# Moving the first two weight pieces of every stage into the stage before, in a two-block transformer kernel on one Trainium2 core

## The reference

```python
x = x + 0.5 * (1.0 + mod[:, 0, 2]) * swiglu(pre(x, 0), ffn_wi[l, 0], ffn_wo[l, 0])
h = pre(x, 1)                       # rmsnorm(x) * g * (1 + scale) + shift
y = hgrn2_mixer(h, ...)             # or diff_attention_mixer, or nsa and gmlp merged
x = x + (1.0 + mod[:, 1, 2]) * y
x = x + 0.5 * (1.0 + mod[:, 2, 2]) * swiglu(pre(x, 2), ffn_wi[l, 1], ffn_wo[l, 1])
```

## Time and profile before

| | us |
|---|---|
| median of 3 runs | 2288.79 |
| lowest and highest run | 2288.27, 2292.33 |
| span of the profiled execution (first to last instruction) | 2286.7 |
| PE busy in it | 2177.3 |
| DVE busy | 1624.0 |
| ACT busy | 1062.8 |

### The profile page before, as it was taken

How to read it: one execution, slowest core, us unless ns; L and a number is a source line. 1 busy time by engine, 2 the same in 40 slices (tenths; PEclk the granted TensorE clock), 3 DMA queues, 4 the chain that set the end, 5 groups by cost and what they waited for, 6 DMA issues and landing times.

```text
span 2286.7 us, 29523 instructions
## 1 busy us (share of the span) xinstructions
PE 2177.3 (95%) x10588; PEld 1802.0 (79%) x10588; DVE 1624.0 (71%) x2258; ACT 1062.8 (46%) x1265; POOL 0.2 (0%) x4
## 2 busy tenths in 40 slices
PE   3999989999999996899999999999999999999998
PEld 2888987788788875788888887778878888777887
DVE  6777767777788785677677866577767776656545
ACT  3344533443534465434443446653354344665334
POOL 0000000000000000000000000000000000000000
PEclk9999999999999997999999999999999999999999
DMA  7899624688688651487678853459867886334553
GB/s 308 317 334 318 218 82 156 231 319 312 228 327 315 226 193 65 149 330 292 229 284 306 315 201 129 131 185 338 302 214 279 309 317 217 129 129 148 191 195 129
DMA packets 128228, 537.20 MB, mean 235 GB/s; under 512 B 15024, under 2 KB 15760, under 8 KB 109200
## 3 DMA queue, kind: packets, MB, share of 16 engines
q1 hardware_dynamic: 128144, 536.06, 65.5%
HBM read 534.90 MB, written 1.10 MB: 234 GB/s over the span
## 4 chain that ended last, share of the span: by engine, by line
PE 87%; DVE 8%; ACT 3%; issue 1%; DMA 1%; SPq 0%; DVEq 0%; ACTq 0%
PE GU L1633 14%; PE GU L1637 14%; PE GU L1635 14%; PE PY L1633 11%; PE PY L1637 11%; PE PY L1635 11%; DVE wL L909 3%; PE TM L1677 2%; ACT wH L517 1%; PE PY L1941 1%; PE PY L2057 1%; ACT M L569 1%; ACT xH L564 1%; DMA M<-in_ada_t 1%; PE PY L1644 1%
## 5 line engine op out<-in xcount | busy, mean ns | idle before, releaser
L909 DVE TENSOR_TENSOR wL<-raw,wH 128x2048 fp32r<-128x2048 f32 x344 | 776.4, 2278 | 232.2 <-ACT wH L517 231.0
L517 ACT ACTIVATE wH<-raw 128x2048 fp32r<-128x2048 f32 x344 | 645.3, 1900 | 149.6 <-PE PY L1637 81.2
L1633 PE MATMUL GU<-wH,xH 128*128 128x512 f32 (+1 forms) x1584 | 628.2, 397 | 34.0 <-DVE xL L1033 30.6
L1637 PE MATMUL GU<-wH,xL 128*128 128x512 f32 (+1 forms) x1584 | 616.3, 389 | 0.0
L1635 PE MATMUL GU<-wL,xH 128*128 128x512 f32 (+1 forms) x1584 | 615.1, 388 | 0.0
L1633 PEld LDWEIGHTS GU<-wH,xH 128*128 128x128 f32 x1584 | 298.3, 188 | 100.1 <-issue 27.4
L1637 PEld LDWEIGHTS GU<-wH,xL 128*128 128x128 f32 x1584 | 298.1, 188 | 62.8
L1635 PEld LDWEIGHTS GU<-wL,xH 128*128 128x128 f32 x1584 | 298.7, 189 | 57.0
L597 ACT ACTIVATE hH<-TM 128x512 fp32r<-128x512 f32 x80 | 47.9, 598 | 587.7 <-PE TM L1677 587.6
L922 DVE CUSTOM_DVE_ANT_0 ada<-ada,cond 128x1024 f32<-128x1024 f32 x272 | 316.6, 1220 | 0.0
L1633 PE MATMUL PY<-wH,hH 128*128 128x512 f32 x640 | 198.6, 392 | 0.9 <-DVE wL L909 0.9
(11 more groups left out here) (288 smaller groups left out, 1888.1 us busy)
## 6 DMA issues: line engine op xcount, KB each, us to landing
raw<-in_up_w SPq DMA_DIRECT2D x352, 512.0 KB, 6.1
ada<-in_ada_t SPq DMA_DIRECT2D x136, 1024.0 KB, 7.8
raw<-in_down_w SPq DMA_DIRECT2D x176, 512.0 KB, 4.8
raw<-in_c_w SPq DMA_DIRECT2D x96, 512.0 KB, 4.4
raw<-in_a_w SPq DMA_DIRECT2D x40, 512.0 KB, 4.6
raw<-in_b_w SPq DMA_DIRECT2D x32, 512.0 KB, 4.5
M<-in_ada_t SPq DMA_DIRECT2D x8, 1024.0 KB, 12.3
gB<-gates SPq DMA_DIRECT2D x12, 512.0 KB, 6.0
```

The costliest lines, as they stand in the source:

```text
L517: act.activation(wH[:, to, 0:words], raw[:, slot, 0:words], ACT.Copy).then_inc(s_high, 1)
L909: dve.tensor_tensor(wL[:, to, 0:words], raw[:, slot, 0:words], wH[:, to, 0:words], ALU.subtract).then_inc(s_split, 1)
L1633: pe.matmul(outs[i], aH, wh[i], start=first, stop=False)
L1637: ins = pe.matmul(outs[i], aL, wh[i], start=False, stop=last)
```

## The change

The first two pieces of a stage get buffers of their own in the arena, `firstH` and `firstL` (two of each, at word 3072 of `M` and up). Their loads, and both cuts, are issued in the preceding stage. For a feed-forward that is one piece in each of its last two turns, for a mixer its end. At the boundary no piece of the new stage is cut any more in tile 0's part. PE turns tile 0 of x inside the last matmuls of the preceding stage (between the halves of `down_last(1)`, or after a quarter of the last tile of a mixer's projection), and tile 1 after group d = 6 instead of 5. DVE does tile 0's modulation before tile 1's `output`, and puts the two halves of that `output` between the blocks of tile 0's `xL`. Since mixers 2 and 3 load other weights into the same words of the arena, that load now also waits until the first two pieces have been used, and stands one piece later.

```diff
+FIRST_AT = 3 * D
+        arena_at = nc.sbuf_base - 4 * ARENA
+        firstH, firstL = ([nc.alloc_sbuf_tensor_at(f"first{part}{q}", [P, PIECE], F32R,
+                                                   offset=arena_at + 4 * (FIRST_AT + (2 * q + k) * PIECE))
+                           for q in range(2)] for k, part in enumerate("HL"))
...
@@ SP: the mixers' other weights
             def load_compression(i):
                 sp.wait_ge(s_x, NT * (3 * i + 7))
+                sp.wait_ge(s_eaten, first_eaten(i + 2))
...
-                    if l > 1 and n == 4:
+                    if l > 1 and n == 5:
                         load_compression(l - 2)
@@ SP: the last two turns of a feed-forward
-                if turns < NF - 1:
-                    loop(1 + turns, NF - 1 - turns, 0)
+                    loop(1, NF - 3, turns > 0)
+                for q in range(2):
+                    c = NF - 2 + q
+                    load_up(l, j, c, 0)
+                    if turns >= c:
+                        load_ada(c0 + c - 1, 0)
+                    if after(l, j):
+                        load_first(after(l, j), q)
+                    load_up(l, j, c, 1)
+                    if turns >= c:
+                        load_ada(c0 + c - 1, 1)
+                    load_down(l, j, c - 1)
                 gate_out(l, j)
                 load_down(l, j, NF - 1)
@@ ACT: a first piece, no wait for a slot of wH
+            def cut_first(q):
+                slot = t.next("piece") % RING
+                act.wait_ge(s_raw[slot], t.next(s_raw[slot], 32))
+                act.activation(firstH[q][:, :], raw[:, slot, :], ACT.Copy).then_inc(s_high, 1)
@@ ACT: norm, at a boundary
+                if before:
+                    squares(0)
+                    root(0)
                 for i in range(NT):
-                    if before:
-                        squares(i)
-                        root(i)
-                    if before and i == 0:
-                        cut(early=before == "ffn")
...
+                    if before and i == 0:
+                        squares(1)
+                        root(1)
@@ ACT: ffn (DVE alike)
                 loop(NF - 3)
+                if after(l, j):
+                    cut_first(0)
                 cut()
                 hidden_high()
...
+                if after(l, j):
+                    cut_first(1)
                 cut()
                 cut()
                 cut_last()
                 hidden_high()
-                if (l, j) != PHASES[-1]:
-                    cut(early=1)
@@ DVE: boundary, tile i
+                    low(0)
+                    low(1)
+                    if before and i == 0:
+                        wait_output_1(before, pieces, 0)
+                        output(1, 0)
+                    low(2)
+                    if before and i == 0:
+                        wait_output_1(before, pieces, 1)
+                        output(1, 1)
+                    low(3)
+                    if before and i == 0:
+                        root(1)
+                        scaled(1)
@@ PE: norm_and_first
-                        if i == 0 and d == 5:
+                        if i == 0 and d == (6 if before else 5):
                             turn_x(1)
@@ PE: the end of a feed-forward, and of a mixer (project_last)
-                down_last(1)
+                down_last(1, 0)
+                if after(l, j):
+                    turn_x(0)
+                down_last(1, 1)
...
+                        if i and h:
+                            token_tile(bank, q, slots[h], i, 512, tiles, range(1))
+                            turn_x(0)
+                            token_tile(bank, q, slots[h], i, 512, tiles, range(1, 4)).then_inc(s_eaten, 1)
```

More of the change, by code:

```diff
@@ L533, in squares @@
                     act.wait_ge(s_in, 16)
[L534 to L541, removed]
+                square_half(i, 0, first)
+                square_half(i, 1, first).then_inc(s_ss, 1)
             def root(i):
@@ L916, in cut_last, with cut_first @@
                 dve.tensor_tensor(lastL[:, :], raw[:, slot, :], lastH[:, :], ALU.subtract).then_inc(s_split, 1)
+            def cut_first(q):
+                slot = t.next("piece") % RING
+                dve.wait_ge(s_high, t.next(s_high))
+                dve.tensor_tensor(firstL[q][:, :], raw[:, slot, :], firstH[q][:, :], ALU.subtract).then_inc(s_split, 1)
             def products(q, piece, free):
@@ L992, in outputs_0, with wait_output_1 @@
                     low_tile(1)
-            def outputs_1(before, pieces):
-                if before == "ffn":
+            def wait_output_1(before, pieces, h):
+                if h:
+                    dve.wait_ge(s_eaten, t.next("done"))
+                elif before == "ffn":
                     dve.wait_ge(s_y, t.next(s_y))
@@ L1000, in outputs_1, with scaled @@
                     dve.wait_ge(s_eaten, t.next("done", pieces - 1))
-                output(1, 0)
-                dve.wait_ge(s_eaten, t.next("done"))
-                output(1, 1)
-            def scaled_identity(i):
+            def outputs_1(before, pieces):
+                for h in range(2):
+                    wait_output_1(before, pieces, h)
+                    output(1, h)
+            def scaled(i):
                 dve.tensor_scalar(diag[:, i, :], ident, rstd[:, i:i + 1], None, ALU.mult).then_inc(s_xn, 1)
@@ L1646, in turn_x, with norm_and_first @@
                         ins.then_inc(s_xt, 1)
-            def norm_and_first(by_tile=False):
-                turn_x(0)
-                slots = [t.next("piece") % RING for _ in range(2)]
+            def norm_and_first(before, by_tile=False):
+                if before is None:
+                    turn_x(0)
+                    slots = [t.next("piece") % RING for _ in range(2)]
+                    high, low = ([w[:, slot, :] for slot in slots] for w in (wH, wL))
+                else:
+                    high, low = ([w[:, :] for w in part] for part in (firstH, firstL))
                 for i in range(NT):
@@ L1744, in ffn @@
                 pe.transpose(TM[0:rows, 1, 0:P], gcol[:, 0:rows], ident).then_inc(s_gt, 1)
+                if after(l, j):
+                    t.next(s_split)
                 up(1)
@@ L2188, in _ @@
                     nsa(l)
+                before = "mixer" if j == 1 else "ffn"
 def table():
```

135 lines of the change are left out of this document (83 added, 52 removed).

## The result

| | before | after |
|---|---|---|
| median of the runs made together (4 each) | 2288.53 us | 2311.02 us |
| lowest, highest of after | | 2310.55, 2314.42 us |
| span of the profiled execution | 2286.7 us | 2308.8 us |
| PE busy | 2177.3 us | 2190.2 us |

The ratio is 1.0101, with a 95% interval of 1.0089 to 1.0114: the change makes the kernel 1% slower. The prediction had 2297.8 us with a range up to 2308, and the time lies 3 us beyond that end. It had the sign, and half of the size.

What follows compares the result with a forecast made beforehand. PE's work and its gaps were taken to bound the kernel. Boundary gains of -10.0, stalls of +16.5 and clock of +2.5 made +9.0 us on a span of 2286.7; with 2.1 us around it, 2297.8 us, range 2280 to 2308.

Steps and rivals of the forecast that it cites:

- What bounds the kernel: PE is 87% of the chain of waits, so a change pays or costs only where gaps on PE close or open.
- The signs that I named: Boundary waits for `xL` under 10 us; five waits of 2 to 4 us behind `hL` or `wL`; ACT waiting for `raw`.
- The schedule of the last two turns: First feed-forward's turns 9 and 10, followed in times: the moved pieces make `hL` reach PE at 220.1, due at 216.83.
- turn 9 absorbs its cut: The first moved cut fits DVE's idle time in turn 9; the pair of cuts ends at 204.6 against 204.45.
- The size of the stall: PE waits 3.3 us for `hL` in the last turn of five feed-forwards that stream `ada_w` to the end: 16.5 us.
- The bounds of 2.1 and 4.3: Stall in us per feed-forward if a piece's transfer takes 2.57 or 3.15 us, in place of 2.9.
- The clock: Granted clock falling behind the five new holes on PE: 0.5 us each, 2.5 us in all, bounds 0 and 12.5.
- the clock falls each time: Rival: full clock price behind every new hole, 12.5 us, giving 2308 us; chance 0.11 together with the gap not closing.
- The gains: Shorter PE waits at boundaries: 5.6 us behind seven feed-forwards and 4.4 us at four mixers' ends, 10.0 us together.
- The rate decides much of this: The DMA rate largely sets the last-turn stall; about 358 GB/s would be 2.93 us a piece and the stall as taken.
- the queue of six pieces: Six pieces of 1.05 MB come down from 185.5 on, at 2.9 us each; the sixth lands at 204.9.
- no stall at all: Rival: spare and idle time suffice in the last turns, so only boundary gains count: 2279 us, down to 2270; chance 0.18.

Runs made afterwards that it cites:

- Experiments 3: Changed kernel with two of DVE's last four products moved behind the hidden product of tile 0, so behind `hL`: 2305.5 us, ratio 1.0074.
- experiment 4: Changed kernel with two of DVE's last four products moved behind tile 0's hidden product, and ACT making `hH` ahead of `cut_last`: 2293.68 us, ratio 1.0027.
- experiment 2: Changed kernel with the first piece still cut in turn 9, but the second cut back at the boundary behind feed-forwards: 2296.87 us, ratio 1.0034.
- experiment 1: Changed kernel with both first pieces behind a feed-forward cut where they were before, behind `cut_last` and at the boundary: 2288.63 us, ratio 1.0.
- experiment 5: Changed kernel with 14 unused matmuls on PE ahead of its wait for `hL` in the five feed-forwards: 2301.66 us, ratio 1.0056.
- Kernel 7: Changed kernel with both first pieces behind a feed-forward loaded behind down(10) and cut in its last turn's tail: 2277.79 us, ratio 0.9952.
- experiment 6: Changed kernel with PE's turn of tile 0 of x put back behind the last matmuls, mixers too: 2327.01 us, ratio 1.0169.

## Why the prediction was right in sign and half in size

**What bounds the kernel**: right. Gaps on PE, and its clock behind them, made the difference; those at `xL` closed, and those at `hL` opened. The signs that I named came: the waits for `xL` at the boundaries fell from 21 to 2.3 us, the five waits for `hL` are there, four inside the 2 to 4 us and one at 4.8, and ACT waits for `raw`.

**The schedule of the last two turns**: right, step by step, in the stage that I followed. Predicted and measured: sixth piece lands 204.9 (ACT takes it at 205.19); its cut ends 209.1 (209.43); up1(10)'s ends 212.0 (212.64); down(9)'s 219.2 (219.74); `hL` ends 219.9 (220.34); ACT ends `hH` at 219.0 (219.56). Experiments 3 and 4 bear out that both chains, DVE's and ACT's, end there. That turn 9 absorbs its cut was right for `hL` in turn 9, and wrong for the kernel: in experiment 2 that one piece costs 8 us against experiment 1.

**The size of the stall**: "I take 3.3: 5 x 3.3 = 16.5 us". Measured 20.3. The first stage is 0.4 longer than I said; the next three are longer still, up to 4.8, and one of them has 0.77 for `wL` besides, which following only the first one could not show. That is 3.8 us. The bounds of 2.1 and 4.3 do not follow from the working either: up1(10) lands six pieces behind the 190.2, so 0.25 us more a piece are 1.5 and 0.33 less are 2.0, which gives about 1.3 and 4.8.

**The clock**, the step that failed: "I take 0.5 us for each of five (one in five pays the full price), 2.5 us". The clock fell behind each of the five holes, and that cost 9.7 us by the traces, 9.4 by experiment 5. That is 7.2 us, the largest miss, and with the 3.8 us of the stalls it carries the time past the range. The one row with such a hole had shown the full price, 2.5 us, and I discounted it because PE had been dense ahead of the new holes. It had, and it did not help. The rival "the clock falls each time" had the mechanism, and 12.5 us for it.

**The gains**: "5.6 + 4.4 = 10.0 us". Kernel 7 has them without the harm: 7.4 us behind the seven feed-forwards and 4.0 in the four mixers, by its timelines. The working was right within 2 us. In the changed kernel the five feed-forwards lose 26.0 us against 20.3 of stalls and 9.7 of clock, so their boundaries gain 4.0, the 0.8 each that I took. The two others gain 1.0 together: there, where I had taken no stall, PE waits 0.19 and 0.85 us for `hL` in the last turn. The four mixers gain 2.9 in place of 4.4, with 1.5 us lost to the clock in the last of them. Together 7.9 us.

**What the stall is made of**: "The rate decides much of this". It decides little of the stall. Of 19.5 us, 3.2 go with seven eighths of the bytes; with three quarters of the bytes and of the cuts' work gone, 16.0 are left for the slot. Each of these sums is from one trace, and traces of kernels that differ only outside these turns have 19.5 and 21.7 (experiment 6), so the cuts' own part can't be told from nothing. My sum had the slot in it ("whose load waited for down(8)'s cut at 202.3") and so came out right, but I put the price on the queue of six pieces. For that reason my range of rates, 2.1 to 4.3 us, said nothing of the true spread. The Trainium skill (DMA: Bandwidth & Descriptors, Specifications) gives about 358 GB/s as one core's limit; the trace does not agree with it as a ceiling, with 423 GB/s in a window above, and it was not what decided.

**The rival "no stall at all"** fell for the changed kernel. It had named what would be needed, free raw buffers and a free queue. The tail has them, and kernel 7 came out at 2277.8, where that rival had 2279.

The sum as measured, by the two profiled spans: 20.3 (stalls) + 9.7 (clock) - 7.9 (boundaries) = 22.1 us.

## What to carry to other kernels

Work moved across a stage boundary is the same amount of work, but not free: ask which slot of which ring it holds, and which load is issued one step later for it. Where two engines' chains end at the same wait, look for a place where both have idle time, rather than shortening one. And price a new hole on TensorE at the hole plus its clock: here 20 us of holes cost 30.

## What the runs showed of the hardware that I had not expected

The length of a hole alone does not tell whether the granted clock falls. It fell behind the changed kernel's holes of 3.4 to 4.8 us, but also behind one of 2.0 us, and stayed up behind one of 3.6 us; both are in the kernel of experiment 4, in windows that begin just behind the hole or in its last 0.6 us:

```profile
778.00:783.00 5.00, 5.00 (x16) 3.97 (x17) 4.78 (x7) 0.21 (x1) 0.00 (x0) 0.66 1.00 370
...
1316.00:1321.00 5.00, 4.46 (x21) 3.69 (x22) 5.00 (x6) 0.64 (x2) 0.00 (x0) 1.00 1.02 399
```

Even the same hole does both. In the first mixer the kernel before has this row and this window:

```profile
391.51 0.50 PE L1633 MATMUL PY<-wH,xH 128*128 128x512 f32 x1 [2.37 <-DVE xL L1131]
...
391.50:396.50 5.00, 4.99 (x22) 4.13 (x23) 3.76 (x4) 0.90 (x3) 0.00 (x0) 1.00 0.85 312
```

And kernel 7:

```profile
391.33 0.80 PE L1718 MATMUL PY<-wH,xH 128*128 128x512 f32 x1 [2.37 <-DVE xL L1211]
...
391.30:396.30 5.00, 4.97 (x16) 4.01 (x17) 4.45 (x3) 2.40 (x3) 0.00 (x0) 0.69 0.87 308
```

What decides it no run here shows. It makes single stages differ by about 1.5 us between traces, as much as a boundary gains.

The Trainium skill (TensorE: Matmul & The Clock Gate, What's actually happening) says that the clock follows how busy PE has been recently, and not a count of instructions. By that rule unused matmuls keep it up, and experiment 5 agrees: 1.00 behind all five holes.
